# Reordering the first stage of a fused block: which engine splits which tile when, and another way to build a table of powers

## The reference

```python
h = rms_norm(x, norm1_g)                       # x: 1024 tokens x 1024
p = h @ w_in                                   # u, v (512 each), s_in (256), gates (2 x 1024)
uv = gelu(p[..., :1024]); s_in = p[..., 1024:1280]
gates = sigmoid(p[..., 1280:] + b_gate)        # g_a, g_b
br_a = gmlp_spatial_gating(u, v, ...)          # layer norm over v, then u * (w_s @ v + b_s)
br_b = s5_mixer(s_in, ...)                     # state-space scan in both directions, gelu, gated
merged = g_a * (br_a @ w_up_a) + g_b * (br_b @ w_up_b)
x = x + merged @ w_out
x = x + expert_choice_ffn(rms_norm(x, norm2_g), ...)   # 16 experts, 128 tokens each
x = rms_norm(x, final_g)
# second block: dilated attention in 3 groups, rg_lru, gated merge, output projection
```

```python
lam_bar = exp(lam * dt); b_bar = (lam_bar - 1) / lam * b
bu = einsum('gph,blgh->blgp', b_bar, u)
states = associative_scan(a*state + bu)        # forward, and backward for the second direction
y = real(einsum('ghp,blgp->blgh', c, states)) + d_skip * u
```

## Time and profile before

| | |
|---|---|
| median of 3 runs | 2941.9 us (2941.42 to 2942.5) |
| the profiled execution's own time | 2942.5 us |
| its span in the profile | 2940.7 us |
| PE busy | 2845.3 us, 97% |
| DVE busy | 1721.0 us, 59% |
| ACT busy | 1283.0 us, 44% |
| POOL busy | 540.1 us, 18% |
| mean granted TensorE clock | 0.99 |

### The profile page before, as it was taken

One profiled execution on the slowest core, in us unless ns is written; L12 is line 12 of the kernel. 1 busy time (PEld: TensorE's weight loads), 2 busy tenths in 40 slices (PEclk: granted clock), 3 DMA queues, 4 the chain that ended last, 5 costly groups with the idle time before them and its releaser, 6 DMA issues. The chain is left out here.

```text
span 2940.7 us, 34626 instructions
## 1 busy us (share of the span) xinstructions
PE 2845.3 (97%) x13278; PEld 2321.3 (79%) x13278; DVE 1721.0 (59%) x1743; ACT 1283.0 (44%) x1408; POOL 540.1 (18%) x276
## 2 busy tenths in 40 slices
PE   7999999979999999999999999999999799999999
PEld 6887778648888888888888877888988687778887
DVE  7952112878888888888888875040312604774132
ACT  4231003237777777777777754030202201434021
POOL 0002222000010110110111122312221322333330
PEclk9999999989999999999999999999999999999999
DMA  4021113389999999999999972111111411111131
GB/s 159 23 54 47 43 43 137 150 342 361 383 381 381 383 374 374 379 380 380 378 379 373 383 270 107 43 55 54 52 49 51 137 44 58 36 47 47 43 129 58
DMA packets 123377, 556.48 MB, mean 189 GB/s; under 512 B 14288, under 2 KB 18416, under 8 KB 90128
## 3 DMA queue, kind: packets, MB, share of 16 engines
q1 hardware_dynamic: 112576, 524.43, 46.5%
q0 software_dynamic: 5360, 20.09, 2.5%
q10 hardware_dynamic: 5344, 10.59, 1.0%
HBM read 521.93 MB, written 32.08 MB: 188 GB/s over the span
## 5 line engine op out<-in xcount | busy, mean ns | idle before, releaser
L2400 DVE TENSOR_TENSOR slots_lo<-buffer,slots_hi 128x2048 fp32r<-128x2048 f32 x384 | 852.6, 2286 | 156.0 <-ACT slots_hi L1724 155.9
L1724 ACT ACTIVATE slots_hi<-buffer 128x2048 fp32r<-128x2048 f32 x384 | 710.2, 1920 | 65.9 <-PE bank L1272 30.1
L976 PE MATMUL bank<-hT_hi,ring_hi 128*128 128x512 f32 x1216 | 485.3, 399 | 5.9 <-ACT buffer L1590 2.6
L978 PE MATMUL bank<-hT_hi,ring_lo 128*128 128x512 f32 x1216 | 474.3, 390 | 0.0
L977 PE MATMUL bank<-hT_lo,ring_hi 128*128 128x512 f32 x1216 | 473.9, 390 | 0.0
L888 POOL TENSOR_TENSOR ring_lo<-buffer,ring_hi 128x1024 fp32r<-128x1024 f32 x111 | 284.7, 2568 | 51.0 <-ACT ring_hi L1503 42.9
L885 POOL CAST ring_hi<-buffer 128x1024 fp32r<-128x1024 f32 x101 | 115.6, 1145 | 874.1 <-DMA buffer<-in_wstream 836.4
L976 PEld LDWEIGHTS bank<-hT_hi,ring_hi 128*128 128x128 f32 x1216 | 228.8, 188 | 59.0 <-DVE hT_lo L2492 7.1
L978 PEld LDWEIGHTS bank<-hT_hi,ring_lo 128*128 128x128 f32 x1216 | 228.5, 188 | 48.3
L977 PEld LDWEIGHTS bank<-hT_lo,ring_hi 128*128 128x128 f32 x1216 | 228.8, 188 | 47.1 <-issue 2.6
L1272 PE MATMUL bank<-slots_hi,xsT_hi 128*128 128x512 f32 x960 | 257.6, 390 | 4.8 <-DVE buffer L2415 4.8
(11 more groups left out here) (456 smaller groups left out, 4158.9 us busy)
## 6 DMA issues: line engine op xcount, KB each, us to landing
buffer<-in_w_gate SPq DMA_DIRECT2D x128, 1024.0 KB, 5.0
buffer<-in_w_up SPq DMA_DIRECT2D x128, 1024.0 KB, 4.8
buffer<-in_w_down SPq DMA_DIRECT2D x128, 1024.0 KB, 8.3
buffer<-in_wstream SPq DMA_DIRECT2D x154, 512.0 KB, 3.6
buffer<-in_x SPq DMA_DIRECT2D x16, 512.0 KB, 7.4
od<-buffer ACTq DMA_DIRECT2D x24, 260.0 KB, 2.1
xacc<-buffer SPq DMA_DIRECT2D x8, 512.0 KB, 2.6
h2d<-buffer SPq DMA_DIRECT2D x8, 512.0 KB, 4.0
```

Source lines behind the costliest of these rows:

```text
L976: mm(bank, lhs[0], rhs[0], start=first, stop=False)
L978: return mm(bank, lhs[1], rhs[0], start=False, stop=last)
L1724: fn(slots_hi[:, n_ % NH, :], slots[n_ % NS], ACT.Copy).then_inc(slot_high_ready, 1)
L2400: tt2(slots_lo[:, place_of(n_), :], slots[n_ % NS], slots_hi[:, n_ % NH, :].bitcast(F32), ALU.subtract).then_inc(slot_split, 1)
```

## The change

The diff has seven edits, in six places of the engines' programs:

1. ScalarE: the high parts of `hT` 0 to 7 and the four squares of x (tokens 512 on) stand in another order: high, square, four times, then the square roots, then the high parts 4 to 7.
2. VectorE: `hT_low(0, 8)` is cut in two, with `tile_low(I_S + 1)` and the normalisation of the second half of x between them; `hT_low(8, 12)` and `hT_low(12, 16)` come later, after the powers and after BBR, BBI.
3. VectorE: `tile_low(I_U + 2)` stands ahead of the table ER, EI, and so does the wait for `sd_stored`; `tile_low(I_U + 3)` comes one doubling earlier.
4. VectorE: the table is doubled from the first entry on with a separately squared factor: seven doublings as before, six squarings (128x16) more, two copies fewer.
5. TensorE and ScalarE: `GB` 0 stands ahead of `KT`, and in the list of banks too.
6. ScalarE: the square root of the layer norm stands right behind the Gelus of v, ahead of the gates; the wait for `C_ready` is gone.
7. Tiles `I_MERGE + 2` and `I_MERGE + 3` are split by POOL, which did nothing there before, rather than by ScalarE and VectorE. The first of them stands behind POOL's two DMAs after `v`.

```diff
--- before.py
+++ after.py
@@ -42,9 +42,9 @@
 I_MOD, I_GATEROW, I_ATT = 38, 54, 62
 I_GATT, I_A2, I_LRU, I_B2, I_WO2, N_STREAM = 98, 102, 114, 130, 146, 154
 
-SPLIT_TILES = [i for i in range(N_STREAM) if i >= I_MERGE + 4 and not I_MOD <= i < I_ATT]
-FRONT_LOW = [I_S, I_S + 1, I_U, I_U + 1, I_U + 2, I_U + 3, I_V, I_V + 1, I_V + 2, I_V + 3] + [I_MERGE + i for i in range(4)]
-FRONT_HIGH = [I_V, I_V + 1, I_U, I_U + 1, I_V + 2, I_V + 3, I_U + 2, I_U + 3] + [I_MERGE + i for i in range(4)]
+SPLIT_TILES = [i for i in range(N_STREAM) if i >= I_MERGE + 2 and not I_MOD <= i < I_ATT]
+FRONT_LOW = [I_S, I_S + 1, I_U, I_U + 1, I_U + 2, I_U + 3, I_V, I_V + 1, I_V + 2, I_V + 3, I_MERGE, I_MERGE + 1]
+FRONT_HIGH = [I_V, I_V + 1, I_U, I_U + 1, I_V + 2, I_V + 3, I_U + 2, I_U + 3, I_MERGE, I_MERGE + 1]
 
 
 
@@ -216,9 +216,9 @@
             b.add((name, f, h), "dve")
 
     gates("GA", 0)
+    gates("GB", 0)
     for j in range(8):
         b.add(("KT", j), "act")
-    gates("GB", 0)
     b.add(("zb", 0), "dve")
     for j in range(8):
         b.add(("z", j), "dve")
@@ -901,6 +901,7 @@
             b1.wait_full(pool, ("v", NT - 1))
             for dst, name in ((wsT, "wsT"), (bsB, "bsB")):
                 pool.dma_start(dst.rearrange("p a b -> p (a b)"), a[name]).then_inc(ln_there, 16)
+            split_tiles(I_MERGE + 2, I_MERGE + 4)
             b1.wait_full(pool, ("y", 3))
             pool.dma_start(wglu.rearrange("p a b -> p (a b)"), a["wglu"]).then_inc(upb_loaded, 16)
             pool.dma_start(upb.rearrange("p a b -> p (a b)"), a["upb"]).then_inc(upb_loaded, 16)
@@ -1101,6 +1102,7 @@
                     feature_tile(b1, ("B", f, h), upb[:, 2 * f:2 * f + 2, :], brB, h, 2)
 
             gates_1("GA", 0)
+            gates_1("GB", 0)
             pe.wait_ge(C_ready, 1)
             for j in range(8):
 
@@ -1120,7 +1122,6 @@
                         last = mm(o, BBI[rows, 8 + m], CI[rows, 8 + m, 8], start=False, stop=True)
                 last.then_inc(full1, 1)
 
-            gates_1("GB", 0)
             pe.wait_ge(ln_there, 16 * 2)
             pe.wait_ge(vn_ready, 4)
             bank = b1.wait_free(pe, ("zb", 0))
@@ -1548,10 +1549,10 @@
                 fn(uT[:, j // 2, (j % 2) * HALF:(j % 2 + 1) * HALF], bank[:], ACT.Gelu).then_inc(drained1["act"], 1)
 
             for j in range(4):
-                hT_high(2 * j, 2 * j + 1)
+                hT_high(j, j + 1)
                 first_square(4 + j)
-                hT_high(2 * j + 1, 2 * j + 2)
             first_roots(1)
+            hT_high(4, 8)
             act.wait_ge(s5_to_act, 2)
             fn(MI[10], MI[8], ACT.Sin).then_inc(act_to_s5, 1)
             fn(MI[11], MI[9], ACT.Sin).then_inc(act_to_s5, 1)
@@ -1588,6 +1589,8 @@
             for tt in range(NT):
                 bank = b1.wait_full(act, ("v", tt))
                 fn(vn[:, tt, :], bank[:], ACT.Gelu).then_inc(drained1["act"], 1)
+            act.wait_ge(bnv_ready, 1)
+            fn(bnsd, bnag[:, :, 1], ACT.Sqrt).then_inc(bns_ready, 1)
 
             def gate_1(name, f, h):
 
@@ -1602,10 +1605,8 @@
                 for h in range(2):
                     gate_1(name, f, h)
 
-            act.wait_ge(C_ready, 1)
             gates_there("GA", 0)
-            act.wait_ge(bnv_ready, 1)
-            fn(bnsd, bnag[:, :, 1], ACT.Sqrt).then_inc(bns_ready, 1)
+            gates_there("GB", 0)
             for j in range(8):
                 d, s, q = j // 4, (j // 2) % 2, j % 2
                 bank = b1.wait_full(act, ("KT", j))
@@ -1613,8 +1614,6 @@
                 dst = KK.rearrange("p (m s) n -> p s m n", s=2)[0:16, s, 4 * q:4 * q + 4, n0:n1]
                 fn(dst, bank[0:16, :].rearrange("p (m n) -> p m n", m=4)[:, :, 0:n1 - n0],
                    ACT.Copy).then_inc(drained1["act"], 1)
-            tile_high(I_MERGE + 2)
-            gates_there("GB", 0)
             for n_ in range(8):
                 h, q = n_ // 4, n_ % 4
                 hs = slice(h * HALF, (h + 1) * HALF)
@@ -1622,7 +1621,6 @@
                     b1.wait_full(act, ("z", 7))
                 act.wait_ge(bra_ready, n_ + 1)
                 fn(bra_hi[:, q, hs], uT[:, q, hs], ACT.Copy).then_inc(bra_high_ready, 1)
-            tile_high(I_MERGE + 3)
             for j in range(4):
                 q, s = j // 2, j % 2
                 bank = b1.wait_full(act, ("y", j))
@@ -2012,9 +2010,10 @@
             x_normal(0)
             tile_low(I_S)
             dve.wait_ge(consts_loaded, 64)
-            hT_low(0, 8)
+            hT_low(0, 4)
+            tile_low(I_S + 1)
             x_normal(1)
-            tile_low(I_S + 1)
+            hT_low(4, 8)
             dve.wait_ge(act_to_s5, 5)
             ea, th_, sh, ch = M[6], M[7], M[10], M[11]
             step(stt(M[13], sh, 2.0, ch, ALU.mult, ALU.mult))
@@ -2062,7 +2061,6 @@
 
                 return x.unsqueeze(2).to_broadcast([P, 16, n_])
 
-            hT_low(8, 12)
             step(v.memset(pR[:, :, 0], 1.0))
             step(v.memset(pI[:, :, 0], 0.0))
             step(v.tensor_copy(pR[:, :, 1], M[17]))
@@ -2072,11 +2070,12 @@
                 complex_multiply(pR[:, :, sh_], pI[:, :, sh_], pR[:, :, sl], pI[:, :, sl],
                                  over(pR[:, :, w_], w_), over(pI[:, :, w_], w_), (16, w_))
 
-            hT_low(12, 16)
+            hT_low(8, 12)
             tile_low(I_U)
             tile_low(I_U + 1)
             complex_multiply(BBR, BBI, s5bc[:, 0], s5bc[:, 1], over(M[20], 16), over(M[21], 16), (16, 16))
 
+            hT_low(12, 16)
             for ri in range(2):
                 for d in range(2):
                     ds_ = slice(8 * d, 8 * d + 8)
@@ -2095,24 +2094,24 @@
                     step(tt2(W_, W_, t1, ALU.add if ri else ALU.subtract))
             v.tensor_copy(M[24], M[23]).then_inc(W_ready, 1)
 
+            tile_low(I_U + 2)
+            dve.wait_ge(sd_stored, 32)
             cur = (M[15], M[13])
             for nxt in ((M[25], M[26]), (M[27], M[28]), (M[29], M[30])):
                 complex_multiply(nxt[0], nxt[1], cur[0], cur[1], cur[0], cur[1], (16,))
                 cur = nxt
-            dve.wait_ge(sd_stored, 32)
             step(v.memset(ER[:, :, 0], 1.0))
             step(v.memset(EI[:, :, 0], 0.0))
-            step(v.tensor_copy(ER[:, :, 1], cur[0]))
-            step(v.tensor_copy(EI[:, :, 1], cur[1]))
+            spare = ((M[25], M[26]), (M[27], M[28]))
             for i in range(7):
                 w_ = 1 << i
-                n_ = min(w_, P - 1 - w_)
-                sl, sh_ = slice(1, n_ + 1), slice(w_ + 1, w_ + 1 + n_)
-                complex_multiply(ER[:, :, sh_], EI[:, :, sh_], ER[:, :, sl], EI[:, :, sl],
-                                 over(ER[:, :, w_], n_), over(EI[:, :, w_], n_), (16, n_))
+                complex_multiply(ER[:, :, w_:2 * w_], EI[:, :, w_:2 * w_], ER[:, :, 0:w_], EI[:, :, 0:w_],
+                                 over(cur[0], w_), over(cur[1], w_), (16, w_))
+                if i < 6:
+                    nxt = spare[i % 2]
+                    complex_multiply(nxt[0], nxt[1], cur[0], cur[1], cur[0], cur[1], (16,))
+                    cur = nxt
                 if i == 4:
-                    tile_low(I_U + 2)
-                if i == 5:
                     tile_low(I_U + 3)
             for i in range(I_V, I_V + 4):
                 tile_low(i)
@@ -2191,7 +2190,6 @@
                    ALU.mult).then_inc(vn_ready, 1)
             b1.wait_drained(dve, ("KT", 7))
             tt2(KK[0:16, :, 112:128], KK[0:16, :, 112:128], Dt[0:16], ALU.add).then_inc(KK_ready, 1)
-            tile_low(I_MERGE + 2)
             dve.wait_ge(ln_there, 16 * 2)
             bank = b1.wait_full(dve, ("zb", 0))
             for q in range(4):
@@ -2213,7 +2211,6 @@
                 hs = slice(h * HALF, (h + 1) * HALF)
                 dve.wait_ge(bra_high_ready, n_ + 1)
                 tt2(bra_lo[:, q, hs], uT[:, q, hs], bra_hi[:, q, hs].bitcast(F32), ALU.subtract).then_inc(bra_split, 1)
-            tile_low(I_MERGE + 3)
 
             def merge_a(f, h):
```

## The result

| | before | after |
|---|---|---|
| median | 2942.2 us (4 runs, 2941.42 to 2943.34) | 2989.58 us (4 runs, 2988.74 to 2991.23) |
| ratio | | 1.0162, 95% interval 1.0144 to 1.0179 |
| span in the profile | 2940.7 us | 2986.8 us |

The change makes the kernel slower by 1.6%, some 47 us. The direction was as forecast (P 0.93); the size was not: 27.6 us were predicted (2969.5 against the 2941.9 known then), up to 34 in the range.

A forecast was written before the change was run, and what follows sets the result against it. TensorE, busy 97%, was taken as the bound, running into VectorE's state-space chain at `GA` 0. Terms 18.4 + 1.7 + 5.9 + 1.7 = 27.7 us gave a 2969.5 us median; range 2963 to 2973, with rivals 2960 to 2976.

The forecast's parts named there:

- parts 1, 2: First low parts reordered, `u_tile(0)` ends 5.5 us late; VectorE stands for `I_U + 2`, so its table starts 9.2 us later.
- part 3: VectorE's table ER, EI: six more squarings, less two copies and a moved low part, add 6.2 us (bounds 5 and 8).
- part 4: POOL's split of `I_MERGE + 2` beside VectorE's last twelve products costs that chain 3.0 us (ends 0 and 3.5).
- part 5: `GB` ahead of `KT`: T comes later, TensorE waits 5.9 us ahead of `y`, and a clock fall costs 1.7 us.
- slow clock at `y` and behind: Behind the wait for T the granted clock falls once more, costing 1.7 us (ends 0 and 1.7).
- for a slow stretch that lasts longer: Allowance in the wider range, 2960 to 2976, for slow clock after 19 us of idling ahead of `GA` 0.
- the clock at 49 us: Behind TensorE's wait in `s_tile(0, 1)`, restart at 49.6, a clock fall costs 1.0 us (ends 0 and 1.7).
- rival D: VectorE's chain does not set `GA` 0: no change, 2942.8 us; chance 0.07, of that 0.02 faster.
- Rival A: POOL's split does not meet VectorE's products or costs little: 3.0 us less, 2966.6 us; chance 0.12.
- Rival B: The wait for T ahead of `y` is hidden: 20.1 us more in place of 27.7, 2962.0 us; chance 0.12.
- rival C: `I_U + 2` is there sooner, VectorE waits only 2.5 us for it: 5.5 us less, 2964.1 us; chance 0.12.
- The rest costs nothing: Moved square root and tile parts cost nothing; loads and splits behind `y` move with TensorE, with no new waits behind 260 us.

The follow-up runs named there:

- experiment 10: Kernel before, with 20 and 8 fp32 products of 128x512 put in the two TensorE waits of the expert routing: 2950.56 us, ratio 1.0023.
- experiment 1: Changed kernel with `KT` ahead of `GB` 0 again: 2962.86 us, ratio 1.0061.
- experiment 2: Kernel before, with only `GB` 0 put ahead of `KT`: 2971.54 us, ratio 1.0094.
- experiment 3: Changed kernel with 26 throwaway products of 128x512 in TensorE's wait for T: 2966.17 us, ratio 1.0076.
- experiment 4: Changed kernel with 24 throwaway products of 128x512 behind the wait for T, ahead of `y`: 2973.28 us, ratio 1.0099.
- experiment 5: Changed kernel with 20 throwaway products of 128x128 in the wait for T: 2965.68 us, ratio 1.0074.
- experiment 9: Changed kernel with `I_MERGE + 2` and `I_MERGE + 3` split by ScalarE and VectorE again, not POOL: 2987.43 us, ratio 1.0152.
- experiment 6: Changed kernel with the table ER, EI doubled as in the kernel before: 2983.55 us, ratio 1.0136.
- experiment 7: Changed kernel with the low part of `I_U + 2` back inside the table, behind its third doubling: 2982.84 us, ratio 1.0137.
- experiment 11: Kernel before, with 10 and 4 products of 128x512 in the two TensorE waits of the expert routing: 2940.94 us, ratio 0.9987.
- experiment 12: As experiment 11, with 12 fp32r products of 128x512 more in the wait ahead of `u_tile(2)`: 2940.51 us, ratio 0.9989 against the kernel before.

## Why the prediction was wrong, step by step

Times in a profile count from the start of its span. TensorE's first product stands at 14.59 in the changed kernel and at 15.25 before, so 0.66 us are added to each difference of starts.

| step | forecast | measured |
|---|---|---|
| `I_U + 2` and the table's start (parts 1, 2) | 9.2 | 77.98 - 70.98 + 0.66 = 7.7 |
| the table (part 3) | 6.2 | 29.81 - 23.94 = 5.9 |
| POOL beside the last products (part 4) | 3.0 | 0.73 + 2.01 = 2.7 |
| `GA` 0 late in all | 18.4 | 174.91 - 159.30 + 0.66 = 16.3 |
| slow clock in `GA` 0 | 1.7 | 52.79 - 44.50 - 6.01 = 2.3 |
| wait for T (part 5) | 5.9 | 6.01 |
| `y` starts late by | 26.0 | 24.6 |
| slow clock at `y` and behind | **1.7** | 19.6 + 2.2 = **21.8** |
| sum | 27.7 | 46.4, of 46.1 + 0.66 |

(52.79 and 44.50 us lie between the first product of `GA` 0 and that of `y`, after and before.)

- The failed step is the last clock term, in part 5: "I expect the clock to fall once more (ends 0 and 1.7)". That it falls was right. Its price was taken from the earlier trace rows, where wide products follow the wait and the level was back after some four microseconds. `y` has only narrow ones. The first stage of the kernel before had no long stretch of narrow products at the lower level, but its trace had one further on, the 8 us from 621 to 629 shown in experiment 10, and it was a warning. The measured term is 21.8 us in place of 1.7. The price of a fall is not a constant: it is half of the time spent at the lower level, and here that lasted until wide products came. That was the whole of `y`, and the upper end should have been `y` at half speed, 24 us more. The forecast took 1.7 us, the upper end of a range from 0 to 1.7, and no rival held more. Experiments 1 to 5 show it from all sides. The range's own allowance "for a slow stretch that lasts longer" was put at `GA` 0, where it cost 0.6 us.
- Without that term the sum is 26.0 against 24.6 measured. Parts 1 and 2 came out 1.5 us lower, and that is luck in part: the clock at 49 us, forecast at 1.0 us, did not fall in the profile of the changed kernel. In that of experiment 9 it did, and VectorE's memset stands at 81.21 rather than 77.98.
- Parts 2, 3 and 4 hold. Experiments 6 and 7 show by their times (6.0 and 6.7 us), and experiment 9 by its trace (2.8 us), that each is paid at TensorE nearly us for us, which rules out rival D. By the Trainium skill, page SBUF — State Buffer, section Who interferes with whom, a VectorE instruction with two SBUF inputs and a GpSimd one that reads SBUF contend, and the port pair they share is an exclusive lock. The trace agrees: POOL's copy and subtraction cost VectorE 0.73 and 2.01 us, and POOL's subtraction lost 3.20 - 2.40 = 0.8 us itself: it began at 159.39, while the first of the two products ran until 160.39. Two products were stretched and not the four or five that the prediction named. Rival A is out.
- Rival B (T's wait hidden) and rival C (`I_U + 2` sooner) are out by the 6.01 and the 7.13 us.
- "The rest costs nothing" holds: no wait behind `y` is new.

The Trainium skill, page TensorE: Matmul & The Clock Gate, section What's actually happening, says that warming up takes a span of time and not a number of products, and counts N=128 products among those that warm the array. For `y` it is not so: 43.6 us of 128x128 products (80 of them, 64 with 64 rows) without a gap stood at 0.50. The measurement decides.

Left open: why wide products raise the level and `y`'s do not. `y` mixes products of 128 rows with such of 64, all narrow and fp32. That they are fp32 is not the reason by itself, as these rows of the kernel before show, with fp32 products of 128x512 (one column of weights) behind a wait:

```profile
594.25 8.72 PE L1238 MATMUL bank<-buffer 128*1 128x512 f32 x16 [3.90 <-DMA buffer<-in_wstream]
```

```profile
596.00:598.00 2.00, 2.00 (x4) 0.26 (x3) 1.90 (x6) 0.00 (x0) 0.00 (x0) 0.50 1.03 422
598.00:600.00 2.00, 2.00 (x6) 0.46 (x5) 1.93 (x5) 0.00 (x0) 0.00 (x0) 0.96 1.05 432
```

The level was back 4 us after they began. Narrowness and the 64 rows were not tried apart. Open too is what decides, beside the length of the wait, whether the clock falls behind one of 3 to 4 us.

## What to carry to other kernels

When an edit makes TensorE wait some microseconds, look at what it does next. If narrow products follow, price the fall of the clock as half of their whole time at the lower level, not as the few us that a neighbouring restart shows. If the wait can't be removed, a few throwaway products that fit into it give the time back; measure one of them first, since a kind that takes twice as long makes the wait longer, and look at the clock behind them: products of 128x128 and 128x512 kept it, the 1x1 column products did not.

A wait ahead of which another engine's chain is late absorbs what TensorE wins or loses before it, so count only what lies behind the last such wait. But the longer wait can let the clock fall, as in experiments 11 and 12, and that is paid behind it.
